# Three edits to VectorE's order in a hybrid linear-attention and latent-attention layer: two more low parts of the input projection, one low part behind a mask, four steps' right factors ahead of the last squared sums

## The chip, the cores and the metric

The kernel runs on one core of one Trainium2 chip. The time is that of the device in microseconds (us); a kernel is run several times and the median counts. The core has five engines that run side by side and meet only at semaphores: TensorE (PE in the profile; its weight loads are PEld), VectorE (DVE), ScalarE (ACT), GpSimd (POOL) and SyncE (SP), which here only issues DMAs.

## The reference, cut to what matters

Everything is float32, 1024 tokens wide 1024.

```python
h = _rmsnorm(x, attn_norm[l])
z = h @ w_in[l]                       # input projection, 1968 columns
# one part of z feeds gated linear attention, chunk by chunk -> o_gla
# the other feeds latent attention with normed and rotated q, k -> o_mla
q = _rmsnorm(q, q_head_norm[l])
k = _rmsnorm(k, k_head_norm[l])
x = x + jnp.concatenate([o_gla, o_mla], axis=-1) @ w_out[l]
h = _rmsnorm(x, mlp_norm[l])
x = x + jnp.square(jax.nn.relu(h @ w_up[l])) @ w_down[l]    # 1024 -> 4096 -> 1024
```

## The kernel before

**Split products.** Each float32 factor is cut in two: a high part, which ScalarE makes by a rounding copy (L1141), and a low part, the factor minus its high part, which VectorE or GpSimd makes by one subtraction. A product is then three matmuls (`split_product`): high by high, high by low, low by high. Whoever makes a low part sets when TensorE may use that factor, and when its raw tile may be loaded anew.

**Input projection.** Its columns are cut into four groups (`IN_GROUPS`, q = 0 to 3). A group multiplies 8 row tiles k of the weight with 8 blocks of 128 tokens; the raw tiles go through a ring of four (`raw`, `RING`), high and low parts through a ring of ten. `low_by_vector(n)`, with n = 8 q + k, says who makes the low part of tile n: true is VectorE (`in_low_parts`, L1769), false is GpSimd (L918). Steps are numbered s = 8 q + b (block b). VectorE makes its low parts of group q + 1 at the last step of group q, ahead of that step's tile (`tile_out`) and of what it does behind it: at s = 23 that is the norm and the turning of the heads of block 6 (`head_norms`: L1691, two at L1697, L1700, L1701). TensorE turns these heads (`behind`, 16 transposes at L2289) after step 24's products.

**Linear attention and output projection.** In the last steps of attention VectorE has a hand-written table, `OUT_LOWS_AT`, of where it makes the low parts of the first output group (`out_low_part`, L1915) among the masks, sums and states of the linear attention (`gla`). A mask is the copy under a causal mask at L1824; TensorE's products with the state wait for both masks of a chunk.

**Up half.** The MLP's two products use Strassen's scheme with seven products (P1, P2, P5, P6, P7, P3, P4, in this order). The up half has `UG` = 8 groups of 512 hidden columns. VectorE forms the sums of its products, squares them (`summed`), and forms sums of squares (`tt`); the results go to ten kinds of staged tiles which SyncE stores to `hidden` in HBM (`hidden_stores(g, which)`, L800).

**Down half.** It has 7 passes of 16 steps t (`D_STEPS` = 112). Step t needs a left factor, loaded by SyncE from `hidden` (`s_all` in the first pass, L821, `l_raw` later, L831), and a right factor from one or two loaded tiles of `w_down` (`r_raw`, L839). VectorE forms the right factor (`down_sum(t)`, into `t_all`), ScalarE rounds both (`dl_hi`, `dr_hi`), GpSimd makes `dl_lo` and VectorE `dr_lo` (`down_low(t)`). TensorE takes four steps as a quad of 48 matmuls, and begins the quad's second, third and fourth step only when their low parts are there. In `down_load(t)` the right tiles of step t wait for `down_low(t - 4)`, and the left tile of steps 10, 12 and 14 waits first for all stores of the groups it reads (`all_stored`; for t = 14 these are all eight groups). All four queues are in order: what stands behind a waiting instruction on its engine waits too. Steps 0 to 7 are already made by VectorE inside the last up group (`down_steps`), steps 8 on after it. The left factor of step 15 in the first pass is the sum of squares that the last line of `up_group` makes (staged kind 6); kind 9 is the square before it.

Of the kernel before, what the change touches and what calls it, by code (L numbers as in the profile page):

```python
# [15 lines left out]
KT = D // P  # L16
# [25 lines left out]
IN_GROUPS, OUT_GROUPS = 4, NH  # L42
# [7 lines left out]
UG = FF // W  # L50
# [16 lines left out]
PAIRS = FF // P // 2  # L67
# [3 lines left out]
D_STEPS = PAIRS * len(PASSES)  # L71
# [15 lines left out]
def layer(nc, x, positions, attn_norm, w_in, w_gate_up, b_gate, gla_out_norm, q_a_norm, w_uq,  # L87
# [9 lines left out]
    with ctx:  # L97
        ctx.enter_context(nc.allow_non_contiguous_dma(reason="gains and positions of a few KB, laid by partition"))

        def sem(name):  # L100
            return ctx.enter_context(nc.semaphore(name))
# [5 lines left out]
        def at(name, shape, offset, dt=F32):  # L107
            return nc.alloc_sbuf_tensor_at(name, shape, dt, offset=base + offset)
# [98 lines left out]
        u_three = at("u_three", [P, 2, W], GB)  # L207
        p_five = at("p_five", [P, 2, W], 84 * KB)
# [122 lines left out]
        p1_out, p5_out, u2_ready, u3_ready = sem("p1_out"), sem("p5_out"), sem("u2_ready"), sem("u3_ready")  # L331
# [43 lines left out]
        def low_by_vector(n):  # L375


            return KT <= n < KT * (IN_GROUPS + 1) and (n >= KT * IN_GROUPS or n % KT in (2, 3, 4, 5))

        def low_made(n):  # L380

# [16 lines left out]
        def staged_as(g, n):  # L398

            if g >= 2:  # L400
                return 9 * g + n - 1
            return g if n == 1 else 8 * g + n
# [123 lines left out]
        STEPS = 6 * MH // 2  # L526
# [101 lines left out]
        def gla_at(d, place):  # L628

            n = GLA_AT[d % 6][place]  # L630
            if n is None or 16 * (d // 6) + n < 0:
                return None
            return divmod(16 * (d // 6) + n, NB)

        @block.sync
        def _(sp):
# [149 lines left out]
            def hidden_stores(g, which):  # L786
                for n in which:
                    kind, pair = STAGED[n]
                    to = h_d[kind, 2 * g + pair]
                    if n < 2:  # L790
                        sp.wait_ge(c11_ready, 2 * g + n + 1)
                    elif n in (2, 4, 6, 7):
                        sp.wait_ge(pairs_ready, 4 * g + {4: 1, 2: 2, 7: 3, 6: 4}[n])
                    else:
                        sp.wait_ge(stage_ready, 6 * g + {3: 2, 5: 3, 8: 5, 9: 6}[n])
                    if n == 0:
                        sp.dma_start(to, keep[:, g % 2, :]).then_inc(keep_stored[g % 2], 16)
                    else:
                        e = staged_as(g, n)
                        sp.dma_start(to, stage[e % STAGES][:, :]).then_inc(stage_stored[e % STAGES], 16)  # L800
# [60 lines left out]
            hidden_stores(UG - 1, (3, 4, 2))  # L861
            for t in range(8, 12):
                down_load(t)
            hidden_stores(UG - 1, (5, 7, 8, 9, 6))

            sp.wait_ge(ulo_done, UP_PRODUCTS)
            for t in range(12, PAIRS):
                down_load(t)

            sp.wait_ge(part_ready, 2 * UP_PRODUCTS)  # L870
# [731 lines left out]
        def _(dve):  # L1602
# [309 lines left out]
            def out_low_part(k):  # L1912
# [3 lines left out]
                                  ALU.subtract).then_inc(wlo_done2, 1)  # L1916


            OUT_LOWS_AT = {(STEPS - 3, 4): 0, (STEPS - 2, 0): 1, (STEPS - 2, 1): 2, (STEPS - 2, 2): 3, (STEPS - 1, 0): 4,
                           (STEPS - 1, 1): 5, (STEPS - 1, 2): 6}  # L1920


# [14 lines left out]
            for d in range(STEPS):  # L1937
                for place in range(5):
# [4 lines left out]
                    if place < 4 and gla_at(d, place):  # L1943
                        gla(*gla_at(d, place))
                    if (d, place) in OUT_LOWS_AT:
                        out_low_part(OUT_LOWS_AT[d, place])
            gla_sums(NB - 1)
# [16 lines left out]
            def tt(out_, in0, in1, op):  # L1964
                return dve.tensor_tensor(out_, in0, in1, op)  # L1965
# [98 lines left out]
            def staged(g, n):  # L2064
                return stage[staged_as(g, n) % STAGES][:, :]

            def stage_free(g, n):
                e = staged_as(g, n)
                if e >= STAGES:
                    dve.wait_ge(stage_stored[e % STAGES], 16 * (e // STAGES))  # L2070
                return staged(g, n)
# [4 lines left out]
            def summed(to, in0, in1):  # L2076
                step(tt(to, in0, in1, ALU.add))
                squared(to, to)

            def made(g, product, i):  # L2080
                dve.wait_ge(part_ready, 2 * turn_of(g, product) + i + 1)
                return ps[:, up_bank(g, product, i), :]

            def up_group(g):
                for i in range(2):
                    u = u_two[:, g % 2, i, :]
                    dve.wait_ge(p1_out, 2 * g + i + 1)
                    tt(u, made(g, P6, i), u, ALU.add).then_inc(u2_ready, 1)
                if g + 1 == UG:
                    down_steps(0, 2)  # L2090
                for i in range(2):
                    dve.wait_ge(u2_ready, 2 * g + i + 1)
                    if g >= 1:
                        dve.wait_ge(stage_ready, 6 * (g - 1) + 4 + 2 * i)
                    tt(u_three[:, i, :], made(g, P7, i), u_two[:, g % 2, i, :], ALU.add).then_inc(u3_ready, 1)
                if g + 1 < UG:
                    up_sums_one(g + 1)
                else:
                    down_steps(2, 4)
                if g == 0:  # L2100

                    dve.wait_ge(x2_stored[NB // 2 - 1], 32)
                for i in range(2):
                    summed(stage_free(g, 2 + i), made(g, P3, i), u_two[:, g % 2, i, :])
                dve.wait_ge(stage_ready, 6 * g + 2)
                tt(stage_free(g, 4), staged(g, 2), staged(g, 3), ALU.add).then_inc(pairs_ready, 1)
                dve.wait_ge(c11_ready, 2 * g + 1)
                tt(staged(g, 2), keep[:, g % 2, :], staged(g, 2), ALU.subtract).then_inc(pairs_ready, 1)
                if g + 1 < UG:
                    up_sums_two(g + 1)  # L2110
                else:
                    down_steps(4, 8)
                for i in range(2):
                    one, two = ((5, 6), (8, 9))[i]
                    summed(stage_free(g, one), made(g, P4, i), u_two[:, g % 2, i, :])
                    dve.wait_ge(p5_out, 2 * g + i + 1)
                    dve.wait_ge(u3_ready, 2 * g + i + 1)
                    summed(stage_free(g, two), u_three[:, i, :], p_five[:, i, :])
                    if i == 0:
                        to = stage_free(g, 7)  # L2120
                        dve.wait_ge(stage_ready, 6 * g + 4)
                        tt(to, staged(g, 5), staged(g, 6), ALU.subtract).then_inc(pairs_ready, 1)
                dve.wait_ge(stage_ready, 6 * g + 6)
                tt(staged(g, 6), staged(g, 6), staged(g, 9), ALU.add).then_inc(pairs_ready, 1)

            def down_sum(t):

                product, f = pass_of(t), t % PAIRS
                own_s, own_t = s_all[f // 4][:, f % 4, :], t_all[f // 4][:, f % 4, :]
                if product == P5 and f in (0, 4, 8):  # L2130

                    dve.wait_ge(part_ready, 2 * (turn_of(UG - 1, (P6, P7, P4)[f // 4]) + 1))
                if product in (P1, P2):
                    dve.wait_ge(*left_landed(t))

                    dve.wait_ge(dllo_done, PAIRS * PASS[{P1: P5, P2: P6}[product]] + f + 1)
                    if product == P1:
                        last = tt(own_s, own_s, left_source(t), ALU.subtract)
                    else:
                        last = tt(own_s, left_source(t), own_s, ALU.subtract)  # L2140
                else:
                    dve.wait_ge(*right_landed(t))
                    if product == P5:
                        last = tt(own_t, right_raw(t, 0), right_raw(t, 1), ALU.subtract)
                    elif product == P7:
                        last = tt(right_raw(t, 0), right_raw(t, 0), right_raw(t, 1), ALU.subtract)
                    else:

                        dve.wait_ge(drlo_done, PAIRS * PASS[{P6: P5, P3: P6}[product]] + f + 1)
                        last = tt(own_t, right_raw(t, 0 if product == P6 else 1), own_t, ALU.subtract)  # L2150
                last.then_inc(d_sum, 1)
# [5 lines left out]
            def down_steps(first, end):  # L2157

                down_sum(first)
                for t in range(first, end):  # L2160
                    if t + 1 < end:
                        down_sum(t + 1)
                    down_low(t)
# [12 lines left out]
            for g in range(UG):  # L2176
                up_group(g)

            down_sum(8)
            for t in range(8, D_STEPS):  # L2180
                if t + 1 < D_STEPS - PAIRS:
                    down_sum(t + 1)
                down_low(t)
                n, f = divmod(t, PAIRS)
                if n >= 1 and f in (8, 10, 12, 14):
                    add_result(n - 1, (f - 8) // 2)
# [468 lines left out]
```

## Time and profile before

| | us |
|---|---|
| median of 3 runs | 1123.13 (1122.3 to 1123.94) |
| the profiled execution's own time | 1125.12 |
| its span, first to last instruction | 1123.4 |
| TensorE (PE) busy in the span | 1103.4 |
| VectorE (DVE) busy | 763.8 |
| GpSimd (POOL) busy | 565.9 |
| ScalarE (ACT) busy | 483.8 |

The profile lists what each engine did and what ended its idle time. Busy time of an engine that others do not wait for costs nothing; what counts is where TensorE, nearly always busy, stands still or runs at a lower granted clock, and who let it go on.

### The profile page before, as it was taken

The page shows a single profiled execution, that of the slowest core. Times are in us where ns is not written, and L with a number is a line of the kernel's source. Part 1 is how long each engine was busy: PE and PEld are TensorE (multiplying, and loading weights), DVE is VectorE, ACT ScalarE, POOL GpSimd, SP SyncE. Part 2 cuts the span into 40 slices and gives each one's busy share as a digit, 9 for nine tenths or more (in the row PEclk, how much of TensorE's full clock was granted, in tenths as well). Part 3 has the DMA queues.
Part 4 walks back from the last instruction along what each step waited for, and adds up shares of the span by engine and source line. Part 5 has one row for each costly group of instructions (what it writes and reads, how often), then busy time and mean ns, then how long its engine had stood idle before and what let it go on. Part 6 is the DMA issues. An engine that isn't in the chain of part 4 may idle for free.

```text
span 1123.4 us, 14304 instructions
## 1 busy us (share of the span) xinstructions
PE 1103.4 (98%) x5190; PEld 890.0 (79%) x5190; DVE 763.8 (68%) x971; ACT 483.8 (43%) x894; POOL 565.9 (50%) x401
## 2 busy tenths in 40 slices
PE   7999999999999999999999999999999999999998
PEld 7988888776666668887888888888878888888887
DVE  5566766675575472387685686568797988888863
ACT  5353544527767742266223332333334443434341
POOL 2332522237878563059545444444554656556562
PEclk8999999999999999999999999999999999999999
DMA  7242523362221152213544333421889693456632
GB/s 251 71 134 67 169 83 113 95 166 60 75 62 52 58 197 84 94 76 100 182 143 138 131 114 122 141 94 57 293 273 364 222 300 101 146 189 218 210 109 85
DMA packets 101717, 158.38 MB, mean 141 GB/s; under 512 B 9360, under 2 KB 43232, under 8 KB 101648
## 3 DMA queue, kind: packets, MB, share of 16 engines
q1 hardware_dynamic: 100032, 152.83, 41.3%
q10 hardware_dynamic: 1296, 4.46, 1.2%
q8 instruction: 42, 0.69, 0.3%
q0 software_dynamic: 320, 0.19, 0.2%
q14 instruction: 27, 0.22, 0.1%
HBM read 115.47 MB, written 41.94 MB: 140 GB/s over the span
## 4 chain that ended last, share of the span: by engine, by line
PE 86%; DVE 6%; POOL 3%; issue 2%; ACT 2%; DMA 1%; SPq 0%; DVEq 0%; ACTq 0%; POOLq 0%
PE ps L2193 83%; PE ps L2289 1%; POOL tx_lo L1098 1%; DVE t_all L1965 1%; DVE dr_lo L1965 1%; POOL p_first L1045 1%; DMA raw<-in_w_in_dram 1%; PE ps L2208 1%; POOL a_lo L1098 1%; POOL ua_lo L1103 1%; DVE m_nm L1890 0%; DVE stage L1965 0%; DVE xn L1612 0%; DVE w_lo L1915 0%; ACT dr_hi L1141 0%
## 5 line engine op out<-in xcount | busy, mean ns | idle before, releaser
L2193 PE MATMUL ps<-dr_hi,dl_hi 128*128 128x512 f32 x448 | 175.1, 391 | 1.6 <-DVE dr_lo L1965 1.6
L1103 POOL TENSOR_TENSOR ua_lo<-up_raw,ua_hi 128x1024 fp32r<-128x1024 f32 x46 | 116.7, 2542 | 116.5 <-ACT ua_hi L1141 116.5
L2193 PE MATMUL ps<-dr_hi,dl_lo 128*128 128x512 f32 x448 | 175.0, 391 | 0.0
L2193 PE MATMUL ps<-dr_lo,dl_hi 128*128 128x512 f32 x448 | 174.9, 390 | 0.0
L1127 POOL TENSOR_TENSOR dl_lo<-l_raw,dl_hi 128x512 fp32r<-128x512 f32 x64 | 102.0, 1621 | 71.5 <-ACT dl_hi L1141 71.0
L1127 POOL TENSOR_TENSOR dl_lo<-s_all,dl_hi 128x512 fp32r<-128x512 f32 x48 | 75.0, 1582 | 58.2 <-ACT dl_hi L1141 57.4
L2193 PEld LDWEIGHTS ps<-dr_hi,dl_hi 128*128 128x128 f32 x448 | 84.5, 189 | 20.2 <-issue 2.8
L2193 PE MATMUL ps<-a_hi,ua_hi 128*128 128x512 f32 x256 | 99.9, 390 | 0.0
L2193 PE MATMUL ps<-a_hi,ua_lo 128*128 128x512 f32 x256 | 99.6, 389 | 0.0
L2193 PE MATMUL ps<-a_lo,ua_hi 128*128 128x512 f32 x256 | 99.6, 389 | 0.0
L2193 PEld LDWEIGHTS ps<-dr_hi,dl_lo 128*128 128x128 f32 x448 | 84.4, 188 | 17.7
L2193 PEld LDWEIGHTS ps<-dr_lo,dl_hi 128*128 128x128 f32 x448 | 84.5, 189 | 17.5
L1141 ACT ACTIVATE ua_hi<-up_raw 128x1024 fp32r<-128x1024 f32 x48 | 50.6, 1058 | 89.9 <-PE ps L2193 79.0
L1965 DVE TENSOR_TENSOR dr_lo<-r_raw,dr_hi 128x512 fp32r<-128x512 f32 x64 | 73.0, 1141 | 11.4 <-ACT dr_hi L1141 11.3
L1045 POOL TENSOR_TENSOR p_first<-p_first,p_ring 128x1024 f32<-128x1024 f32 (+3 forms) x40 | 70.6, 1765 | 16.8 <-PE ps L2193 13.4
L2193 PE MATMUL ps<-wi_hi,a_hi 128*128 128x512 f32 (+1 forms) x192 | 76.0, 396 | 2.7 <-DVE a_lo L1623 2.6
L1141 ACT ACTIVATE dl_hi<-l_raw 128x512 fp32r<-128x512 f32 x64 | 39.8, 622 | 82.5 <-PE ps L2193 78.9
L2193 PE MATMUL ps<-tx_hi,ua_hi 128*128 128x512 f32 x192 | 74.7, 389 | 0.0
L2193 PE MATMUL ps<-tx_lo,ua_hi 128*128 128x512 f32 x192 | 74.7, 389 | 0.0
L2193 PE MATMUL ps<-tx_hi,ua_lo 128*128 128x512 f32 x192 | 74.7, 389 | 0.0
L1965 DVE TENSOR_TENSOR dr_lo<-t_all,dr_hi 128x512 fp32r<-128x512 f32 x48 | 58.8, 1240 | 22.5 <-ACT dr_hi L1141 22.1
L2193 PE MATMUL ps<-wi_hi,a_lo 128*128 128x512 f32 (+1 forms) x192 | 73.9, 385 | 0.0
(264 smaller groups left out, 2575.9 us busy)
## 6 DMA issues: line engine op xcount, KB each, us to landing
r_raw<-in_w_down_dram SPq DMA_DIRECT2D x144, 256.0 KB, 3.5
hidden<-stage SPq DMA_DIRECT2D x72, 256.0 KB, 2.0
up_raw<-in_w_up_dram SPq DMA_DIRECT2D x16, 1024.0 KB, 5.5
l_raw<-hidden SPq DMA_DIRECT2D x64, 256.0 KB, 3.4
raw<-in_w_in_dram SPq DMA_DIRECT2D x24, 256.0 KB, 3.5
z_gla<-z_stage SPq DMA_DIRECT2D x16, 256.0 KB, 2.0
raw<-in_w_out_dram SPq DMA_DIRECT2D x16, 256.0 KB, 2.9
xs<-in_x_dram SPq DMA_DIRECT2D x8, 512.0 KB, 7.3
```

The lines of the kernel that those rows point to most:

```text
L1045: pool.tensor_tensor(total, total, p_tile(j)[:, :, seen], ALU.add).then_inc(sum_done, 1)
L1098: pool.tensor_tensor(lo, t_new[n][:, :, :], hi.bitcast(F32), ALU.subtract).then_inc(tlo_done, 1)
L1103: pool.tensor_tensor(ua_lo[n % UP_RING][:, :, :], up_source(g, product), ua_hi[n % UP_RING][:, :, :].bitcast(F32), ALU.subtract).then_inc( ...
L1127: pool.tensor_tensor(slot(dl_lo, t), left_source(t), slot(dl_hi, t).bitcast(F32), ALU.subtract).then_inc(dllo_done, 1)
L1141: return act.activation(dst, src, ACT.Copy, scale=scale)
L1965: return dve.tensor_tensor(out_, in0, in1, op)
L2193: return pe.matmul(dst, lhsT, rhs, start=start, stop=stop, skip_group_check=onto)
L2208: last = pe.transpose(bank4(4 + j)[:, i, :], src[:, (4 * j + i) * P:(4 * j + i + 1) * P], ident[:, :])
L2289: last = pe.transpose(bank4(4 + i // 4, DQK)[:, i % 4, :], m_qk[:, b % 2, i, :], ident[:, :])
```

## The change

There are three edits, and none adds or removes arithmetic.

1. In the fourth group of the input projection (n = 24 to 31) the low parts of k = 6 and 7 go from GpSimd to VectorE, so that VectorE makes six there instead of four.
2. In the output projection's table, low part 3 goes from place 2 of its step to place 3, which is behind the second mask.
3. In the last up group, steps 8 to 11 of the down half are made ahead of the last squared sum and the last sum of squares. SyncE's order follows: the loads of steps 12 and 13 go ahead of the stores of kinds 9 and 6.

```diff
         def low_by_vector(n):
-            return KT <= n < KT * (IN_GROUPS + 1) and (n >= KT * IN_GROUPS or n % KT in (2, 3, 4, 5))
+            return KT <= n < KT * (IN_GROUPS + 1) and (n >= KT * (IN_GROUPS - 1) and n % KT >= 2 or n >= KT * IN_GROUPS or n % KT in (2, 3, 4, 5))
...
-            hidden_stores(UG - 1, (5, 7, 8, 9, 6))
+            hidden_stores(UG - 1, (5, 7, 8))
             sp.wait_ge(ulo_done, UP_PRODUCTS)
-            for t in range(12, PAIRS):
+            for t in range(12, 14):
+                down_load(t)
+            hidden_stores(UG - 1, (9, 6))
+            for t in range(14, PAIRS):
                 down_load(t)
...
-            OUT_LOWS_AT = {(STEPS - 3, 4): 0, (STEPS - 2, 0): 1, (STEPS - 2, 1): 2, (STEPS - 2, 2): 3, (STEPS - 1, 0): 4,
+            OUT_LOWS_AT = {(STEPS - 3, 4): 0, (STEPS - 2, 0): 1, (STEPS - 2, 1): 2, (STEPS - 2, 3): 3, (STEPS - 1, 0): 4,
...
+            def up_last_sum(g, i, two):
+                dve.wait_ge(p5_out, 2 * g + i + 1)
+                dve.wait_ge(u3_ready, 2 * g + i + 1)
+                summed(stage_free(g, two), u_three[:, i, :], p_five[:, i, :])
...
                     summed(stage_free(g, one), made(g, P4, i), u_two[:, g % 2, i, :])
-                    dve.wait_ge(p5_out, 2 * g + i + 1)
-                    dve.wait_ge(u3_ready, 2 * g + i + 1)
-                    summed(stage_free(g, two), u_three[:, i, :], p_five[:, i, :])
                     if i == 0:
+                        up_last_sum(g, i, two)
...
+                if g + 1 == UG:
+                    down_steps(8, 12)
+                up_last_sum(g, 1, 9)
                 dve.wait_ge(stage_ready, 6 * g + 6)
                 tt(staged(g, 6), staged(g, 6), staged(g, 9), ALU.add).then_inc(pairs_ready, 1)
...
-            down_sum(8)
-            for t in range(8, D_STEPS):
+            down_sum(12)
+            for t in range(12, D_STEPS):
```

Line numbers below that of the loads are 3 higher in the changed kernel (L1769 becomes L1772, L1965 becomes L1968). On VectorE, at the end of the third group of the input projection (`wi_lo` are the low parts, `z_stage` the tile of step 23, `m_qk` to `m_rs` the heads of block 6), there stood before:

```order
L1745 TENSOR_REDUCE h_ss_214<-m_sq_65 128x16
L1769 TENSOR_TENSOR wi_lo_56<-raw_51,wi_hi_55 128x512 x4
L1612 SCALAR_TENSOR_TENSOR z_stage_83<-tanh_g_85,ps 128x512
L1612 SCALAR_TENSOR_TENSOR z_stage_83<-z_stage_83,gn_88 128x512
L1691 TENSOR_TENSOR m_qk_64<-m_qk_64,h_rs_215 128x1536
L1697 TENSOR_TENSOR m_rc_68<-m_qk_64,r_cos_66 128x512
L1697 TENSOR_TENSOR m_rs_69<-m_qk_64,r_sin_67 128x512
```

and in the changed kernel:

```order
L1748 TENSOR_REDUCE h_ss_214<-m_sq_65 128x16
L1772 TENSOR_TENSOR wi_lo_56<-raw_51,wi_hi_55 128x512 x6
L1615 SCALAR_TENSOR_TENSOR z_stage_83<-tanh_g_85,ps 128x512
L1615 SCALAR_TENSOR_TENSOR z_stage_83<-z_stage_83,gn_88 128x512
L1694 TENSOR_TENSOR m_qk_64<-m_qk_64,h_rs_215 128x1536
L1700 TENSOR_TENSOR m_rc_68<-m_qk_64,r_cos_66 128x512
L1700 TENSOR_TENSOR m_rs_69<-m_qk_64,r_sin_67 128x512
```

Two more low parts stand ahead of the tile and of the heads; on GpSimd the pair of them is gone.

On VectorE, from the end of the last up group to the down half's step 12 (`t_all2` with `dr_lo0` are steps 8 to 11, `t_all3` with `dr_lo1` steps 12 to 15, `stage4` the first sum of P4's second half, `stage5` kind 9, `stage2` kind 6), there stood before:

```order
L1612 SCALAR_TENSOR_TENSOR stage4_177<-stage4_177 128x512
L1965 TENSOR_TENSOR stage5_178<-u_three_170,p_five_171 128x512
L1612 SCALAR_TENSOR_TENSOR stage5_178<-stage5_178 128x512
L1965 TENSOR_TENSOR stage2_175<-stage2_175,stage5_178 128x512
L1965 TENSOR_TENSOR t_all2_185<-r_raw_188 128x512 x2
L1965 TENSOR_TENSOR dr_lo0_195<-t_all2_185,dr_hi0_191 128x512
L1965 TENSOR_TENSOR t_all2_185<-r_raw_188 128x512
L1965 TENSOR_TENSOR dr_lo0_195<-t_all2_185,dr_hi0_191 128x512
L1965 TENSOR_TENSOR t_all2_185<-r_raw_188 128x512
L1965 TENSOR_TENSOR dr_lo0_195<-t_all2_185,dr_hi0_191 128x512
L1965 TENSOR_TENSOR t_all3_186<-r_raw_188 128x512
L1965 TENSOR_TENSOR dr_lo0_195<-t_all2_185,dr_hi0_191 128x512
```

and in the changed kernel:

```order
L1615 SCALAR_TENSOR_TENSOR stage4_177<-stage4_177 128x512
L1968 TENSOR_TENSOR t_all2_185<-r_raw_188 128x512 x2
L1968 TENSOR_TENSOR dr_lo0_195<-t_all2_185,dr_hi0_191 128x512
L1968 TENSOR_TENSOR t_all2_185<-r_raw_188 128x512
L1968 TENSOR_TENSOR dr_lo0_195<-t_all2_185,dr_hi0_191 128x512
L1968 TENSOR_TENSOR t_all2_185<-r_raw_188 128x512
L1968 TENSOR_TENSOR dr_lo0_195<-t_all2_185,dr_hi0_191 128x512 x2
L1968 TENSOR_TENSOR stage5_178<-u_three_170,p_five_171 128x512
L1615 SCALAR_TENSOR_TENSOR stage5_178<-stage5_178 128x512
L1968 TENSOR_TENSOR stage2_175<-stage2_175,stage5_178 128x512
L1968 TENSOR_TENSOR t_all3_186<-r_raw_188 128x512 x2
L1968 TENSOR_TENSOR dr_lo1_196<-t_all3_186,dr_hi1_192 128x512
```

The three instructions on `stage5` and `stage2` went behind all eight of steps 8 to 11, and now stand ahead of the sum of step 12, which stood ahead of step 11's low part.

On SyncE's queue at the same place (`stage1`, `3`, `4` are kinds 5, 7, 8) there stood before:

```order
L800 DMA hidden<-stage4_177 128x512
L800 DMA hidden<-stage5_178 128x512
L800 DMA hidden<-stage2_175 128x512
L821 DMA s_all3_182<-hidden 128x512
L839 DMA r_raw_188<-in_w_down_dram 128x512 x2
L821 DMA s_all3_182<-hidden 128x512
L839 DMA r_raw_188<-in_w_down_dram 128x512 x2
L821 DMA s_all3_182<-hidden 128x512
```

and in the changed kernel:

```order
L800 DMA hidden<-stage4_177 128x512
L821 DMA s_all3_182<-hidden 128x512
L839 DMA r_raw_188<-in_w_down_dram 128x512 x2
L821 DMA s_all3_182<-hidden 128x512
L839 DMA r_raw_188<-in_w_down_dram 128x512 x2
L800 DMA hidden<-stage5_178 128x512
L800 DMA hidden<-stage2_175 128x512
L821 DMA s_all3_182<-hidden 128x512
```

The two stores now stand directly ahead of the loads of step 14.

## Rows read from the trace of the kernel before

**Rows 1.** PE's waits, whole span: us in total, times, longest.

```profile
PE ps L2193 <- DVE a_lo L1623: 2.6, 1, 2.6
...
PE ps L2193 <- DVE dr_lo L1965: 1.6, 2, 1.4
...
PE ps L2193 <- POOL wi_lo L918: 1.1, 2, 0.7
```

**Rows 2.** Timeline of DVE, steps 23 and 24: start, us, what.

```profile
192.18 2.50 DVE L1769 TENSOR_TENSOR wi_lo<-raw,wi_hi 128x512 fp32r<-128x512 f32 x4 [2.80 <-ACT wi_hi L1141]
194.59 0.68 DVE L1612 SCALAR_TENSOR_TENSOR z_stage<-tanh_g,ps 128x512 f32<-128x512 f32 x1
...
195.92 1.75 DVE L1691 TENSOR_TENSOR m_qk<-m_qk,h_rs 128x1536 f32<-128x1536 f32 x1
197.71 1.78 DVE L1697 TENSOR_TENSOR m_rc<-m_qk,r_cos 128x512 f32<-128x512 f32 x1
```

**Rows 3.** Timeline of ACT, same place: high parts of k = 6 and 7.

```profile
196.95 1.27 ACT L1141 ACTIVATE wi_hi<-raw 128x512 fp32r<-128x512 f32 x2 [3.24 <-DMA raw<-in_w_in_dram]
```

**Rows 4.** Timeline of POOL, same place: their low parts.

```profile
197.66 2.97 POOL L918 TENSOR_TENSOR wi_lo<-raw,wi_hi 128x512 fp32r<-128x512 f32 x2 [5.00 <-ACT wi_hi L1141]
```

**Rows 5.** Timeline of PE, same place.

```profile
198.19 0.39 PE L2193 MATMUL ps<-a_hi,wi_lo 128*128 128x512 f32 x1
...
202.03 1.95 PE L2289 MATMUL ps<-ident,m_qk 128*96 128x128 f32 x16 [0.38 <-DVE m_qk L1701]
```

**Rows 6.** Timeline of DVE, the same chain for block 7.

```profile
210.40 1.76 DVE L1691 TENSOR_TENSOR m_qk<-m_qk,h_rs 128x1536 f32<-128x1536 f32 x1 [0.22 <-POOL h_rs L907]
212.19 0.69 DVE L1697 TENSOR_TENSOR m_rc<-m_qk,r_cos 128x512 f32<-128x512 f32 x1
...
213.86 0.42 DVE L1701 TENSOR_TENSOR m_qk<-m_rs,m_rc 128x256 f32<-128x256 f32 x1
```

**Rows 7.** Windows: stretch, busy us (instructions) by engine, PEclk, DMA, GB/s.

```profile
12.65:18.20 5.55, 5.55 (x15) 5.18 (x16) 4.44 (x7) 3.56 (x8) 4.40 (x7) 0.50 0.87 299
837.50:841.00 3.50, 3.50 (x10) 2.75 (x9) 2.66 (x3) 1.25 (x3) 3.38 (x3) 0.52 0.73 233
```

**Rows 8.** Timeline of DVE, second mask of the last chunk.

```profile
404.32 0.43 DVE L1824 COPY_PREDICATED sc<-causal,ps 128x256 f32<-128x256 int32 x1
```

**Rows 9.** Timeline of PE, the output projection's last row tile.

```profile
412.96 0.47 PE L2193 MATMUL ps<-w_hi,a_hi 128*128 128x512 f32 x1 [0.32 <-DVE w_lo L1915]
```

**Rows 10.** Timeline of DVE, end of the up half.

```profile
825.97 0.69 DVE L1965 TENSOR_TENSOR stage<-u_three,p_five 128x512 f32<-128x512 f32 x1
...
828.02 1.28 DVE L1965 TENSOR_TENSOR t_all<-r_raw 128x512 f32<-128x512 f32 x2
...
836.34 0.68 DVE L1965 TENSOR_TENSOR dr_lo<-t_all,dr_hi 128x512 fp32r<-128x512 f32 x1
```

**Rows 11.** Timeline of PE, third and fourth quad of the down half.

```profile
832.85 0.39 PE L2193 MATMUL ps<-dr_hi,dl_hi 128*128 128x512 f32 x1
...
833.30 0.39 PE L2193 MATMUL ps<-dr_hi,dl_lo 128*128 128x512 f32 x1
...
835.96 0.47 PE L2193 MATMUL ps<-dr_hi,dl_hi 128*128 128x512 f32 x1 [1.36 <-DVE dr_lo L1965]
...
847.71 0.39 PE L2193 MATMUL ps<-dr_hi,dl_hi 128*128 128x512 f32 x1
```

**Rows 12.** Timeline of SP, loads of steps 14 to 16: issue, us.

```profile
834.60 0.33 SPq L821 DMA_DIRECT2D s_all<-hidden  x1
...
838.37 0.33 SPq L831 DMA_DIRECT2D l_raw<-hidden  x1
```

**Rows 13.** Tile stage, SP, 827.3 to 828.6 us: stores of kinds 9 and 6.

```profile
DMA to landing us min/median/max: 3.5/3.5/3.6
```

**Rows 14.** Tile r_raw, SP, 835.5 to 838.2: loads of steps 14 and 15.

```profile
DMA to landing us min/median/max: 3.1/4.8/5.9
```

**Rows 15.** Tile l_raw, SP, 838.2 to 838.8: the load of step 16.

```profile
DMA to landing us min/median/max: 5.8/5.8/5.8
```

## The prediction

> **What bounds the kernel now.** I read the table of busy times first: TensorE is busy 1103.4 of 1123.4 us, so the other engines matter only where they let it stand. Next its waits [rows 1]: of the three longest, one lies at the very start (2.6 us for `a_lo`). The other two lie where the change works: 1.1 us for GpSimd's low parts of the input projection, and 1.6 us for `dr_lo` at the start of the down half. Third, for each edit, I read the timelines of TensorE and of its feeders over the same 10 to 20 us, to see which chain ends last and what stands in that chain's queue. Fourth, the granted clock by windows: a wait can cost more than its length. After the first wait the clock stood at 0.50 for 5.55 us, after the second at 0.52 for 3.5 us, which is 1.2 GHz instead of 2.4 [rows 7].
>
> **Edit 1, two more low parts on VectorE.** Before: VectorE makes four low parts (2.50 us, 0.63 each), then the tile of step 23 at 194.59, then from 195.92 the heads of block 6 [rows 2]. ScalarE makes the high parts of k = 6 and 7 only from 196.95 to 198.22, since their raw tiles land then [rows 3]. GpSimd follows from 197.66 to 200.63 [rows 4]. TensorE has the rest of step 24 done at 198.19; with 0.23 us for that matmul and six more of the same for k = 6 and 7 it would be ready for the heads at 199.8. Held by the low parts and last by the heads, it begins their transposes at 202.03 [rows 5].
>
> After: VectorE's queue is in order and all six low parts stand ahead of the tile and the heads. The two new ones can't start before their high parts, and those hang on a transfer that nothing in the change moves. VectorE idles from 194.7, makes k = 6 from 197.6 and k = 7 from 198.22 to 198.85. TensorE gets both in time (it wants k = 6 at 198.4 and k = 7 at 199.1), so the 1.1 us of waiting for GpSimd goes. What is late next is the heads: tile of step 23 at 198.85, 1.33 us for it (195.92 less 194.59), heads from 200.2. Their chain took 6.1 us before (195.92 to 202.03), with two multiplications that ran beside GpSimd's low parts and took 1.78 us each [rows 2]; for block 7, with GpSimd idle, the same shape took 0.69 us and the chain 3.88 us (210.40 to 214.28) [rows 6]. I take 3.88: the heads end at 204.06 and TensorE starts them at 204.1. That is 2.1 us later than 202.03, after 4.3 us of standing idle.
>
> The Trainium skill, "SBUF — State Buffer", Who interferes with whom, says that a VectorE instruction with two SBUF inputs and a GpSimd one that reads SBUF hold a shared port in turn, and one blocks the other. By it the chain is 3.88 us as taken; were the 1.78 us those instructions' own, it would be 6.1 us and the transposes would start at 206.3.
>
> Next the clock. The stand of 4.3 us is longer than either of those after which it fell to half [rows 1, 7]. At half speed a stretch loses half its length: 2.8 us for the first, 1.7 us for the second. The second came out of dense matmuls as this one does, so I take 1.7 us; ends 0 and 2.8. The Trainium skill, "TensorE: Matmul & The Clock Gate", The HAM clock gate, says that an idle TensorE falls to 1.2 GHz and only activity brings 2.4 GHz back. By it this stand costs more than its own length; without such a rule edit 1 costs 2.1 us.
>
> Edit 1: +3.8 us, between +2.1 and +4.9. TensorE's next wish from VectorE, the heads of block 7, moves with it: VectorE's chain for them begins with block 6's transposes, so the shift isn't caught up.
>
> **Edit 2, the low part behind the mask.** The mask ran at 404.32 behind two low parts [rows 8]; it now runs one low part sooner and TensorE's products with the state may start a little earlier. But TensorE then waits anyway for the last low part of the same output group, at 412.96 with 0.32 us [rows 9], and that part stands behind the same low parts and high parts as before. What is gained ahead of it is waited there. I take 0; between -0.6 and +0.6, one low part alone (0.63) each way.
>
> **Edit 3, four steps ahead of the last sums.** Before: the three instructions on kinds 9 and 6 take 2.05 us (825.97 to 828.02), steps 8 to 11 follow, and step 11's low part ends at 837.02 [rows 10]. TensorE's third quad begins at 832.85; matmuls follow each other in 0.226 us (833.30), 48 of them in 10.9 us, so it should end at 843.7. It ends at 847.71 [rows 11]: 4.0 us lost, of which 1.7 at the low clock [rows 7] and the rest standing for steps 10 and 11.
>
> After: all of steps 8 to 11 come 2.05 us sooner. Step 10 is there at 833.9 and is wanted at 834.2. Step 11, which also loses step 12's sum ahead of it (0.6), is there at 834.4 and wanted at 834.9. That quad doesn't stand: -4.0 us, and the fourth begins at 843.7.
>
> What is late next is the load of step 14. Its left tile may be loaded only when every store of the up half has landed. Before, the last store was issued at 828.1, landed 3.5 us later [rows 13], and nobody waited: SyncE came to step 14 at 834.60 [rows 12]. Now kind 6 is made after step 11: 834.4 plus 2.05 us, and one of the three beside GpSimd's low part of step 12 (1.1 more as above) or not; I take 837.0. Its store lands at 840.6, and only then SyncE issues step 14's left tile (+6 us) and behind it, at 841.0 and 841.4, the two right tiles. The loads of steps 14 and 15 took 3.1 to 5.9 us to land, median 4.8 [rows 14]; for step 14, alone in the queues, I take 4.0: 845.4. On VectorE step 14's sum stands ahead of step 13's low part, so that is ready at 846.8, and TensorE wants it at 844.4: 2.4 us. Step 15's second tile, issued at 842.7 with 4.8 us, lands at 847.5; step 14's low part behind its sum is ready at 848.8, 1.3 us after TensorE wants it. Step 16's tile, issued 843.2 instead of 838.37 [rows 12], takes 5.8 us [rows 15]; its sum stands ahead of step 15's low part, which is ready at 850.4: 0.9 us more. Together 4.6 us of standing, and again 1.7 us at half clock. Edit 3: -4.0 + 4.6 + 1.7 = +2.3 us. With all landings at 3.1 us the stands shrink to 1.6 us without a fall of the clock: -2.4. With 5.9 us they are 6.0: +3.7. Later quads start 2.3 us late while their loads start 5 us late. I take it that they still fit, since TensorE has no listed wait for a low part in the passes that follow [rows 1]; what that leaves open is inside the bounds.
>
> **The sum.** 3.8 + 0 + 2.3 = +6.1 us. The profiled execution took 1125.12 us, its span and 1.7 us around it, 2.0 us above the median of the runs. A profiled run would so take 1131.2 us, and the median of plain runs 1129.2 us.
>
> **The rivals.**
> - *Step 14 in time.* The last stores find emptier queues, GpSimd doesn't get in the way, and the loads land before TensorE asks; edit 3 keeps its 4.0 us. For it: 3.1 us is among the landings [rows 14]. Against it: store and load now lie end to end, and even 3.1 us leaves a stand. With edit 1: 3.8 - 4.0 = -0.2, 1122.9 us.
> - *The clock holds.* TensorE's stands cost only their length: 2.1 + 0.6 = +2.7, 1125.8 us. For it: the 1.1 us of waits at 199 us left no mark. Against: both longer waits did [rows 7].
> - *The port isn't the reason.* The heads' chain stays at 6.1 us whatever GpSimd does: 2.2 us more, 1131.4 us. Against it: 0.69 us in rows 6.
> - *Faster: the heads aren't in the way.* If the two tiles landed some 3 us sooner, VectorE would pass without a stop (six low parts end at 195.9), GpSimd's 1.1 us would go and the heads would be ready before TensorE is: up to 2.2 us gained (202.03 to 199.8), with edit 3's 4.0 us 1116.9 us. It decides at a landing before about 195. Against: ScalarE stood 3.24 us for the transfer [rows 3], and SyncE's order there is the same.
>
> **How the numbers follow.** The forecast has 0.54, step 14 in time 0.18, the clock holds 0.12, the port 0.08, the faster case 0.08. The measurement can tell 0.2%, 2.2 us: 1120.9 and 1125.4 are the borders. Faster: the last case, 0.08. Same: step 14 in time, and a third of the clock's case, 0.22. Slower: the rest, 0.70. The bounds of the three edits sum to -0.9 and +9.2; with the rivals I set 1122.5 to 1132.0. The forecast's own range is 1126 to 1132.
>
> **What would show it.** In the profile after: six low parts in VectorE's rows with an idle of about 3 us for ScalarE's `wi_hi` between the fourth and fifth; `m_rc` at 0.69 us; transposes at 204 with an idle of 4 us put down to `m_qk`, and a window below 1.00 behind them. At the third quad no wait for `dr_lo`; at the fourth, waits for `dr_lo` at steps 13 to 15, VectorE idle for `r_raw`, SyncE's load of step 14 some 3.5 us behind the last store. I am wrong if VectorE's two new low parts start before 197 us, if TensorE's transposes start by 202, or if the fourth quad runs through.

## The result and the profile after

The changed kernel took 1134.38 us, median of 4 runs (1132.22 to 1134.87); the kernel before took 1123.54 us beside it, median of 4 (1122.3 to 1124.52). The ratio is 1.0094, 95% interval 1.0081 to 1.0107: slower by 10.8 us. The forecast was 1129.2 us, with a range up to 1132.0. The direction was right, the size was not: the time lies 2.4 us above the range.

The profiled execution took 1134.87 us (before: 1125.12), with a span of 1133.1 us (before: 1123.4). TensorE's busy time rose from 1103.4 to 1108.4 us for the same number of matmuls. So of the 9.75 us that the profiled execution is longer, half is matmuls that took longer and half is standing. First TensorE's waits (us in total, times, longest), to be read beside [rows 1]:

```profile
PE ps L2299 <- DVE m_qk L1704: 4.1, 1, 4.1
PE ps L2203 <- DVE dr_lo L1968: 4.0, 2, 2.1
PE ps L2203 <- DVE a_lo L1626: 2.7, 1, 2.7
...
PE ps L2203 <- DVE w_lo L1918: 0.7, 1, 0.7
```

The wait for GpSimd's `wi_lo` is gone; in its place stands one of 4.1 us for `m_qk`, the heads. The waits for `dr_lo` grew from 1.6 to 4.0 us.

**The first place, steps 23 and 24.** The timeline of VectorE (start, us, what; to be read beside [rows 2]):

```profile
192.42 2.50 DVE L1772 TENSOR_TENSOR wi_lo<-raw,wi_hi 128x512 fp32r<-128x512 f32 x4 [2.80 <-ACT wi_hi L1144]
197.91 1.32 DVE L1772 TENSOR_TENSOR wi_lo<-raw,wi_hi 128x512 fp32r<-128x512 f32 x2 [3.00 <-ACT wi_hi L1144]
199.15 0.68 DVE L1615 SCALAR_TENSOR_TENSOR z_stage<-tanh_g,ps 128x512 f32<-128x512 f32 x1
...
200.48 1.75 DVE L1694 TENSOR_TENSOR m_qk<-m_qk,h_rs 128x1536 f32<-128x1536 f32 x1
202.26 0.69 DVE L1700 TENSOR_TENSOR m_rc<-m_qk,r_cos 128x512 f32<-128x512 f32 x1
```

VectorE stands 3.0 us behind its fourth low part. ScalarE's high parts of k = 6 and 7 wait for their raw tiles as in [rows 3]:

```profile
197.25 1.26 ACT L1144 ACTIVATE wi_hi<-raw 128x512 fp32r<-128x512 f32 x2 [3.30 <-DMA raw<-in_w_in_dram]
```

The heads begin at 200.48 instead of 195.92 and then run in 3.9 us instead of 6.1: `m_rc` takes 0.69 us where it took 1.78 beside GpSimd's low parts [rows 2, 4]. TensorE's timeline, beside [rows 5]:

```profile
204.41 3.65 PE L2299 MATMUL ps<-ident,m_qk 128*96 128x128 f32 x16 [4.09 <-DVE m_qk L1704]
207.71 0.78 PE L2203 MATMUL ps<-a_hi,wi_hi 128*128 128x512 f32 x1
```

The transposes start 2.4 us later by the traces' own times, 2.2 beyond the 0.2 us by which this execution was already behind. Then the same sixteen take 3.65 us instead of 1.95. The windows (as [rows 7]) show why, there and at two later places:

```profile
204.30:209.60 5.30, 5.19 (x21) 4.65 (x22) 2.16 (x5) 3.18 (x4) 0.00 (x0) 0.50 0.18 44
...
261.00:265.00 4.00, 3.95 (x15) 2.09 (x15) 0.28 (x1) 2.87 (x6) 2.33 (x2) 0.57 0.30 95
...
853.00:861.00 8.00, 5.85 (x15) 4.26 (x16) 6.02 (x7) 3.58 (x7) 4.50 (x3) 0.63 1.02 394
```

The granted clock is 0.50 for 5.3 us behind the wait at 204 us. It is 0.57 at 261 to 265 us, at the start of the attention, where the kernel before kept 1.00:

```profile
256.00:260.00 4.00, 3.91 (x21) 2.33 (x21) 0.31 (x2) 3.51 (x8) 3.90 (x2) 1.00 0.33 97
```

TensorE's waits there are the same in both, for `m_nm`. Before, then after:

```profile
256.09 0.27 PE L2434 MATMUL ps<-ident,m_nm 128*8 128x128 f32 x1 [0.79 <-DVE m_nm L1890]
```

```profile
261.05 0.38 PE L2444 MATMUL ps<-ident,m_nm 128*8 128x128 f32 x1 [0.79 <-DVE m_nm L1893]
```

**The last place, steps 12 to 16 of the down half.** SyncE (beside [rows 12]), then VectorE (beside [rows 10]), then TensorE (beside [rows 11]):

```profile
843.43 1.05 SPq L800 DMA_DIRECT2D hidden<-stage  x2
846.36 0.32 SPq L821 DMA_DIRECT2D s_all<-hidden  x1
846.74 0.90 SPq L839 DMA_DIRECT2D r_raw<-in_w_down_dram  x2
```

```profile
839.48 1.47 DVE L1968 TENSOR_TENSOR dr_lo<-t_all,dr_hi 128x512 fp32r<-128x512 f32 x2
840.87 1.81 DVE L1968 TENSOR_TENSOR stage<-u_three,p_five 128x512 f32<-128x512 f32 x1
...
851.45 0.69 DVE L1968 TENSOR_TENSOR t_all<-r_raw 128x512 f32<-128x512 f32 x1 [5.32 <-DMA r_raw<-in_w_down_dram]
852.06 0.68 DVE L1968 TENSOR_TENSOR dr_lo<-t_all,dr_hi 128x512 fp32r<-128x512 f32 x1
```

```profile
852.89 0.47 PE L2203 MATMUL ps<-dr_hi,dl_hi 128*128 128x512 f32 x1 [1.89 <-DVE dr_lo L1968]
855.97 0.77 PE L2203 MATMUL ps<-dr_hi,dl_hi 128*128 128x512 f32 x1 [2.15 <-DVE dr_lo L1968]
```

The third quad runs without a stop. Behind it the two stores, the left tile that waits for their landing, and the right tiles follow end to end; VectorE stands 5.3 us for the first right tile, and TensorE stands twice.

When each matmul's start is compared with that of the same matmul before, TensorE's delay grows like this: 0.2 us from the start, 4.7 at 204 to 210 us, 1.5 at 261 to 265, nothing at the mask (0.3 us gained there are waited for at `w_lo`), -4.0 in the third quad and +7.35 in the fourth. That makes 9.75 us.

### The profile page after: what moved, and what is told of

Read it like the earlier page. It is cut to its first block, busy times and chain, and to the rows that moved or that the text cites. A ratio compares the mean times of both kernels' runs of the same rounds, so it can differ in the third digit from the quotient of the medians.

```text
span 1133.1 us, 14304 instructions
## 1 busy us (share of the span) xinstructions
PE 1108.4 (98%) x5190; PEld 894.1 (79%) x5190; DVE 757.0 (67%) x973; ACT 484.0 (43%) x894; POOL 562.8 (50%) x399
## 4 chain that ended last, share of the span: by engine, by line
PE 85%; DVE 6%; POOL 2%; issue 2%; ACT 2%; DMA 2%; SPq 0%; DVEq 0%; ACTq 0%
PE ps L2203 82%; PE ps L2299 1%; POOL tx_lo L1101 1%; DMA raw<-in_w_in_dram 1%; DVE t_all L1968 1%; DVE dr_lo L1968 1%; DVE stage L1968 1%; PE ps L2218 1%; POOL a_lo L1101 1%; DVE m_nm L1893 1%; POOL ua_lo L1106 1%; DMA r_raw<-in_w_down_dram 0%; DVE xn L1615 0%; ACT dr_hi L1144 0%; ACT a_hi L1144 0%
## 5 line engine op out<-in xcount | busy, mean ns | idle before, releaser
L1968 DVE TENSOR_TENSOR dr_lo<-r_raw,dr_hi 128x512 fp32r<-128x512 f32 x64 | 70.3, 1099 | 12.9 <-ACT dr_hi L1144 12.9
L2203 PE MATMUL ps<-wi_lo,a_hi 128*128 128x512 f32 (+1 forms) x192 | 73.9, 385 | 0.0
```

What stands on the lines that cost most here:

```text
L2203: return pe.matmul(dst, lhsT, rhs, start=start, stop=stop, skip_group_check=onto)
```

## The experiments

Each kernel ran in five rounds, interleaved with the kernel before on the same chip, which took a median of 1124.08, 1124.17, 1124.12 and 1123.9 us in the four comparisons. All differences below are medians against the one beside it.

### One edit at a time

**Edit 1 alone** is the kernel before with the new `low_by_vector` line.

> Edit 1 alone. Theory (VectorE's queue holds the heads of block 6 behind two low parts that hang on a transfer, and TensorE's stand then costs clock): transposes of the heads some 4.9 us later seen from six matmuls behind them (4.7 in the changed kernel's trace), so +4.7 us, and +6.2 if the fall of the clock in the attention stage (1.5 us, at 261 us in the changed kernel) comes with it. Rival (most of the loss is edit 3's): at most +2.5 us. Rival (edit 1 is harmless, since GpSimd's waits of 1.1 us go): 0 or below.

Measured: 1127.76 us, +3.7; ratio 1.0038 [1.0024, 1.0052]. The wait for `m_qk` is 4.1 us as in the whole change, and the clock in the windows of 2 us from 202 to 210 us is 0.65, 0.50, 0.50 and 0.64. The one stop makes the cost.

**Edit 2 alone** is the one moved entry of `OUT_LOWS_AT`.

> Edit 2 alone, the low part behind the mask. Theory: 0 within 0.6 us, with the wait for the last low part of the output group (0.32 us before, 0.7 in the changed kernel) longer by what is gained ahead of it. Rival: it carries a part of the loss, +1 us or more.

Measured: 1124.0 us, -0.1; ratio 0.9999 [0.999, 1.0008]. It costs nothing that can be told.

**Edit 3 alone** is everything else in the diff.

> Edit 3 alone. Theory (the third quad's 4.0 us are gained and the fourth quad stands for the loads behind the stores): +3.3 us, with waits for dr_lo of 1.9 and 2.2 us in the fourth quad and the clock at half behind them. Rival (the stand in the fourth quad came from edit 1's shift of the whole pipeline): the fourth quad runs through and the time is 3 to 4 us below before.

Measured: 1127.57 us, +3.5; ratio 1.0035 [1.0023, 1.0047]. Its two stands in the fourth quad come to 4.9 us:

```profile
844.69 0.47 PE L2203 MATMUL ps<-dr_hi,dl_hi 128*128 128x512 f32 x1 [1.55 <-DVE dr_lo L1968]
848.95 0.77 PE L2203 MATMUL ps<-dr_hi,dl_hi 128*128 128x512 f32 x1 [3.32 <-DVE dr_lo L1968]
```

**Edit 1 with the two late low parts behind the heads** keeps all six on VectorE:

```
-                    in_low_parts(s // NB + 1)
+                    in_low_parts(s // NB + 1, range(6))
                 tile_out(s)
                 behind(s)
+                if s % NB == NB - 1:
+                    in_low_parts(s // NB + 1, range(6, KT))
```

> Edit 1 with the two new low parts behind the tile of step 23 and the heads of block 6 instead of ahead of them; all six still on VectorE. Theory (it is the order in VectorE's queue that costs): the heads end about 199.8, the low parts at 200.4 and 201.0, TensorE waits about 2 us for k = 6 and 0.5 for k = 7 and starts the heads by 201.9: within 0.5 us of before, if the clock holds. Rival (two more low parts are too much for VectorE here wherever they stand): as edit 1 alone, +4.7 us or more.

Measured: 1124.16 us, +0.1; ratio 1.0006 [0.9997, 1.0014]. The heads run in the time in which VectorE stood, with `m_rc` at 0.69 us, and TensorE now waits for VectorE's low part instead (the line below). The clock did not hold in the profiled execution: it is 0.57 from 200 to 204 us, and the place costs 1.5 us there, which the median of the runs doesn't show.

```profile
199.50 0.50 PE L2195 MATMUL ps<-a_hi,wi_hi 128*128 128x512 f32 x1 [1.88 <-DVE wi_lo L1769]
```

So six low parts on VectorE are not too many. What costs is that two which can't start yet stand ahead of the heads in a queue that runs in order.

### Do the edits add up?

The single edits make +7.2 us, the whole change made +10.8. The changed kernel ran again, beside one that leaves edit 2 out of it (and so differs from it in the mask's place alone).

> The changed kernel once more, beside the single edits' parts. Edit 1 alone measured +3.7 us and edit 3 alone +3.5 us over the kernel before, edit 2 nothing, which makes +7.2; the changed kernel measured +10.8 in another comparison. Theory A (the edits add up, and the rest was the share of executions in which the clock also falls at the attention around 256 us and at the third quad, 1.5 to 1.7 us each): +6.5 to +8.5 here. Theory B (the three together cost something that none of them costs alone): +10 to +11.5 again.

Measured: 1133.01 us, +8.8; ratio 1.0077 [1.0058, 1.0096]. It lies between the two theories.

> Edits 1 and 3 without the moved mask. If the mask's edit costs only in company (the output projection's wait for w_lo is 0.7 us in the changed kernel, 0.3 before), this is 0.5 to 3.5 us under the changed kernel. If the interaction, or chance, is between edits 1 and 3 alone, it is within 1 us of it.

Measured: 1131.67 us, +7.5; ratio 1.0069 [1.0052, 1.0087]. That is 1.3 us under the changed kernel, where the first expectation put it, but the two intervals overlap, and in both profiles of the changed kernel the mask's place gains 0.3 us and gives it back at `w_lo`. So edit 2 can't be told from nothing. In this comparison the edits add up within the intervals. The first comparison's +10.8 stands higher, at 9.1 to 12.0 us, from four runs of which three have a mean clock of 0.991 or less. Time follows the clock: each run's record has a mean granted clock, and since the clock was either 1.00 or 0.50, a mean of 0.989 is some 25 us at half clock and one of 0.995 some 11 us. Of the 90 runs of the kernel before in these four comparisons, the 8 at 1.000 have a median of 1122.1 us, the 23 at 0.998 one of 1122.7, the 35 at 0.997 one of 1124.1, the 3 at 0.996 one of 1124.4 and the 21 at 0.995 one of 1125.2. The changed kernel's ten runs read the same way: two at 0.995 took 1130.1 and 1130.8 us, two at 0.994 took 1131.8 and 1132.2, one at 0.991 took 1134.0, five at 0.989 took 1134.2 to 1135.1. In the second profile of this same kernel (1131.84 us) the attention kept its clock, though its waits for `m_nm` are the same; the two windows, first profile, then second:

```profile
260.00:266.00 6.00, 5.21 (x21) 2.82 (x20) 1.27 (x2) 4.82 (x9) 3.59 (x2) 0.72 0.35 98
```

```profile
256.00:260.00 4.00, 2.75 (x19) 2.04 (x19) 2.30 (x4) 3.18 (x7) 1.34 (x1) 1.00 0.61 178
260.00:264.00 4.00, 3.96 (x19) 2.08 (x20) 0.10 (x1) 3.94 (x6) 3.75 (x3) 1.00 0.32 100
```

Over the fourteen profiles of this study the clock fell at the attention in three (the changed kernel once, edit 2 alone, one of edit 3's variants), in each at unchanged waits. Behind the third quad's 1.4 us wait it fell in three of the six profiles that have this wait (the kernel before among them, edit 1's and edit 2's alone not). Behind the stand of 4 us at the heads it fell in all four profiles that have it, and at edit 3's stands in the fourth quad in seven of eight; the eighth is the one below where the stand there shrank to 1.0 us.

How long it stayed low differs too. At the heads it was back at 1.00 by 207 us in the changed kernel's second profile and in that without edit 2, where the place cost 3.8 and 3.6 us in all; in the first profile and with edit 1 alone it stayed low until 209 us and more, and the place cost 4.7 and 4.9. In the fourth quad it stayed low for some 7 us in all four profiles of edit 3 as it stands (the changed kernel twice, edit 3 alone, edits 1 and 3). At the heads and in the fourth quad of the second profile:

```profile
203.00:207.00 4.00, 3.74 (x18) 3.54 (x19) 1.03 (x3) 1.91 (x3) 0.00 (x0) 0.57 0.00 0
207.00:210.00 3.00, 3.00 (x15) 2.45 (x14) 2.84 (x3) 2.96 (x3) 0.07 (x1) 1.00 0.80 202
852.00:859.00 7.00, 6.17 (x15) 4.85 (x16) 7.00 (x8) 4.03 (x7) 4.76 (x3) 0.51 1.03 398
```

There is also a place which no kernel of this study changed. At the first wait of [rows 1] the clock fell in all fourteen profiles. It was still 0.50 from 17 to 18 us in five of the fourteen profiles, the kernel before and the changed kernel's first among them; in the other nine it was back at 1.00 by 17.2 us, and TensorE was 1.0 to 1.3 us further on at 20 us.

### Mending edit 1

ScalarE makes tiles 2 to 5 of the fourth group ahead of its tanh of step 23. Their raw buffers come free sooner, and so do the loads of tiles 6 and 7:

```
+                    if q == 2 and b == NB - 1:
+                        for k in range(2, KT - 2):
+                            in_high_part(q + 1, k)
...
-                        for k in range(0, 2) if b == 0 else range(2, KT):
+                        for k in range(0, 2) if b == 0 else range(KT - 2 if q == 2 else 2, KT):
```

> Edit 1 with ScalarE's high parts of the fourth group, tiles 2 to 5, ahead of its tanh of the third group's last step, so that the buffers of raw tiles 6 and 7 come free and their loads are issued some 2 us sooner. Theory A (the stand of the heads is VectorE waiting for the high part of tile 7, which waits for its load): VectorE does not stop, the heads' transposes start at 202 us or sooner, and the whole is -2 to +1 us against the kernel before. Theory B (six low parts and the heads are too much work for VectorE there anyway): the transposes still wait over 3 us, and it is +3 us or more.

Measured: 1121.56 us, -2.6; ratio 0.9976 [0.9964, 0.9987]. The high parts of tiles 6 and 7 come at 192.86 and 193.75 us instead of from 196.95 on. VectorE stands 1.9 and 0.2 us for them and begins the tile of step 23 at 195.03, and the transposes start 1.8 us sooner than before:

```profile
193.52 0.69 DVE L1772 TENSOR_TENSOR wi_lo<-raw,wi_hi 128x512 fp32r<-128x512 f32 x1 [1.86 <-ACT wi_hi L1141]
194.42 0.69 DVE L1772 TENSOR_TENSOR wi_lo<-raw,wi_hi 128x512 fp32r<-128x512 f32 x1 [0.20 <-ACT wi_hi L1141]
```

```profile
200.28 1.95 PE L2292 MATMUL ps<-ident,m_qk 128*96 128x128 f32 x16 [0.47 <-DVE m_qk L1704]
```

The same without edit 1 tells whose gain that is.

> The kernel before with ScalarE's high parts of tiles 2 to 5 ahead of tanh, without edit 1. With edit 1 it measured -2.6 us. Theory A (edit 1's two low parts on VectorE are worth something once the tiles are early: the 1.1 us that TensorE waits for GpSimd and the 1.78 us of shared port): -0.5 to +0.5 us here. Theory B (all of the gain is the earlier tiles, and edit 1 is worth nothing): -2 to -3 us here too.

Measured: 1121.93 us, -2.2; ratio 0.9984 [0.9976, 0.9993]. Theory B holds: the gain is the earlier tiles' own; what edit 1 adds to it, 0.4 us, can't be told from nothing. Last, the whole change with this one thing added:

> The whole change, with ScalarE's high parts of tiles 2 to 5 ahead of tanh as the one thing added; edits 2 and 3 stay as they are. The changed kernel measured +10.8 and +8.8 us in its two comparisons, the sum of the single edits is +7.2. Theory A (edit 1's cost is all in the one stop of VectorE for the two late tiles, and the edits add up): the transposes of block 6's heads wait under 1 us, edit 3's cost alone is left, +0 to +3 us against before. Theory B (the edits cost more in company wherever the first stop is): +4 to +7 us.

Measured: 1125.42 us, +1.5; ratio 1.0016 [1.0007, 1.0026], as by theory A. TensorE waits 0.5 us at most for the heads. One stop less takes back 7.3 us of the 8.8 measured last for the whole change; edit 1's cost alone and the mending's own gain make 5.9 (3.7 + 2.2), which is within the intervals. Edit 3's stands are all there still: TensorE's two waits for `dr_lo` come to 4.5 us.

### Mending edit 3

First only the order on SyncE's queue:

```
+            for t in range(14, PAIRS):
+                down_load(t, left=False)
             hidden_stores(UG - 1, (9, 6))
             for t in range(14, PAIRS):
-                down_load(t)
+                down_load(t, right=False)
```

> Edit 3 with one more thing changed: SyncE issues w_down's right tiles of steps 14 and 15 ahead of the last two stores instead of behind them. Theory A (VectorE stands for r_raw of step 14 for 5.3 us because its load is issued behind the stores, which wait for the last sums): no wait for r_raw over 1 us, no wait of TensorE over 1 us in the fourth quad, and the gain of the third quad is kept: -1 to -4 us against the kernel before. Theory B (the loads are slow at this point wherever they are issued, or the left tiles of the last step are what is late): +1 to +4 us, with the waits on other steps.

Measured: 1127.35 us, +3.2; ratio 1.0027 [1.0017, 1.0036]. The time is theory B's, in its second form. Of theory A only one sign came: VectorE no longer stands for `r_raw`, but ScalarE stands for the left tile, which still waits for the last store to land, and it is in ScalarE's queue ahead of the high parts that VectorE needs:

```profile
842.33 0.63 ACT L1146 ACTIVATE dl_hi<-s_all 128x512 fp32r<-128x512 f32 x1 [3.62 <-DMA s_all<-hidden]
```

Step 14's left tile is of pair 0, whose store is long done. Next it waits for that alone and goes ahead of the two stores, with its right tiles and those of step 15:

```
+                    if f == PAIRS - 2:
+                        e = staged_as(UG - 1, 4)
+                        sp.wait_ge(stage_stored[e % STAGES], 16 * (e // STAGES + 1))
-                    if f % 2 == 0 and f >= 10:
+                    elif f % 2 == 0 and f >= 10 or f == PAIRS - 1:
                         all_stored(f // 2 + 1)
```

> Edit 3 with step 14 taken out of the last stores' way: its left tile (sum kind, pair 0) waits for its own store alone instead of every store, and SyncE issues it and the right tiles of steps 14 and 15 ahead of the last two stores; only step 15's left tile stays behind them. With the right tiles alone moved ahead, edit 3 still cost +3.2 us, and ScalarE stood 3.6 us for step 14's left tile. Theory A (what costs is the chain last sum, store, landing, left tile, end to end): now TensorE waits for dr_lo under 1 us in the fourth quad, the third quad's gain is kept, -1.5 to -4 us against before. Theory B (the end of the up half and the start of the down half share the transfer queues, which are full from 844 us on, so that something is late in any order): +1 to +4 us.

Measured: 1124.65 us, +0.5; ratio 1.0001 [0.9991, 1.001], between the two theories. Most of the cost is gone, but the gain isn't there: TensorE still stands 1.0 us at step 15, whose left tile does hang on the last store, and 1.0 us more at 859.35 us, in the next quad.

```profile
847.24 0.47 PE L2207 MATMUL ps<-dr_hi,dl_hi 128*128 128x512 f32 x1 [1.03 <-DVE dr_lo L1972]
```

> Edit 1 with the high parts ahead, and edit 3 with step 14 not held; edit 2 left out. If both mendings hold and add up: -4 to -6.5 us against before, and no wait of TensorE for m_qk or dr_lo over 1 us. If only the first holds: -2 to +1 us.

Measured: 1123.11 us, -1.0; ratio 0.9994 [0.9985, 1.0004]: only the first mending holds. The second adds nothing to it: here step 15 stood for 2.5 us and the clock fell to 0.50 at 848 us. The best kernel of the study is edit 1 with the high parts ahead, at -2.6 us.

## Why the forecast fell short

- **Edit 1, the stand: right.** Predicted: idle for `wi_hi` between the fourth and fifth low part, `m_rc` at 0.69 us, transposes 2.1 us late. Measured: 3.0 us of idle, 0.69 us, 2.2 us. With GpSimd idle `m_rc` took 0.69 us here and in the kernel with the heads first. The Trainium skill ("SBUF — State Buffer", Who interferes with whom) says that such a VectorE instruction contends with a GpSimd one that reads SBUF; the traces agree, with 1.78 us beside GpSimd's low parts.
- **Edit 1, "I take 1.7 us" for the clock: mis-sized.** It measured 2.5 us (4.7 in all). The longer stand was followed by 5.3 us at half clock and more, not by 3.5 as in [rows 7]. The bounds held it. In two other profiles of the same stand the place cost 3.6 and 3.8 us in all, which is what was forecast; so the term is a choice between two sizes, and which one comes differs from execution to execution.
- **The clock at the attention: missing.** The sum had no term for a place that the change doesn't touch. There the clock fell in the profiled execution, 1.5 us. The prediction had taken "the clock fell" and "the clock stayed" of one profile as a property of the place; for short waits it is a property of the execution.
- **Edit 2: right**, at nothing. What was gained ahead is waited for at `w_lo` (0.7 instead of 0.32 us).
- **Edit 3: the mechanism right, the size off.** Predicted -4.0, stands of 4.6, clock 1.7: +2.3. Measured -4.0 and +7.35: +3.35. There were two stands, 4.0 us together, and not three, so the rest, 3.3 us, is mostly the clock: the window from 853 to 861 us has 0.63, and TensorE ran at half clock from 855.97 to some 861.8 us, which by the clock alone is 2.9 us. The clock term was again the one too small, in all four profiles of edit 3 as it stands. That the stands came out near the forecast is in part luck: the last sum ended 0.7 us later than forecast (at 844.13 us, which without the 6.4 us of delay up to there is 837.7, forecast 837.0), and the last store landed in 2.0 us and not in 3.5. The -4.0 is that of one profile as well. In the three profiles of kernels with the old order whose clock held at the third quad (edit 1 alone, edit 2 alone, edit 1 with the high parts ahead) that quad lost 2.3 to 2.4 us instead of 4.0, so edit 3 has less to gain there in such an execution.
- **From the profile to the median: wrong by 1.5 us.** The prediction took 2.0 us off, since the profile of before stood that far above its median. That profile had the fall at the third quad and the long one at the start, which other executions don't have. The profile of after stood only 0.5 us above its median.

So the step that failed is the price of the clock. The prediction took 1.7 us a stand from one stretch of [rows 7]; the profile shows 2.5 us at the heads and about 3 us in the fourth quad. It took nothing for the attention, where the fall cost 1.5 us. And it took the falls of one execution for a fixed 2.0 us above the median, where after the change it was 0.5. In the profile the terms miss 0.9 + 1.5 + 1.05 us, with 0.2 from the start; the way to the median misses 1.5. Together that is the 5.2 us between 1129.2 and 1134.38.

Of the rivals, the one that said "faster, if the two tiles landed some 3 us sooner" was right about what decides: with the tiles' high parts some 4 us sooner, edit 1 is no loss. "The clock holds" is refuted by every profile with the stand of 4 us at the heads, "step 14 in time" by the two stands in the fourth quad, and "the port isn't the reason" by `m_rc` at 0.69 us. Left open is why the changed kernel spends more executions at 0.989 to 0.991 than its parts do (edit 1 alone has 0.992 to 0.997, edit 3 alone 0.994 to 0.997). Added up, the medians' losses against 0.997 (0.0025 and 0.002) give some 0.9925. That a stop at 204 us makes the fall at 261 us likelier would fit, but none of the runs shows it.

## What to carry to other kernels

In a queue that runs in order, ask of each instruction that is added when its own input lands, not how long it takes: two low parts, 1.3 us together, let the heads begin 4.6 us later, and the same two behind the heads cost +0.1 us (interval -0.3 to +1.6). A store whose landing a load waits for is best issued as early as it can be; to move work ahead of it buys a gain here and gives it back one quad later. And one profile doesn't tell what a short wait costs when the clock may or may not fall behind it: take the run-to-run spread of the clock into the range.

## What was not expected of the hardware

- Equal waits with unequal clocks: at the attention (0.44 and 0.79 us) and at the third quad (1.4 us) the clock fell to 0.50, for 3 to 4 us, in some executions and stayed at 1.00 in others. The kernel before spans 1121.9 to 1129.0 us over 90 runs, and most of that follows the mean clock.
- The length of the half-clock stretch isn't fixed: 5.3 us and more behind the 4.1 us stand in one profile of the changed kernel, while the other profile of it was back at full speed by 207 us. The start of the kernel, the same in all fourteen profiles, has both lengths too.
- The last two stores landed in 2.0 and 2.1 us, less than the 3.5 us assumed from [rows 13], and the load that waits for them was issued 2.2 us after the second (846.36 less 844.16). The `r_raw` loads issued between 840 and 860 us took a median of 5.5 us to land. The DMA share is 0.81 from 847 to 853 us and 1.0 from 853 to 870 us, at some 400 GB/s.
